# A two-pass decoder layer on eight cores: embedding-stage adds on Pool, new buffer places, a norm and the start loads moved

## What is computed

```python
def rmsnorm(x, g):
    return x * rsqrt(mean(x * x, axis=-1) + EPS) * g

def swiglu(x, w_gate, w_up, w_down):              # D_MODEL 1024, D_FF 2816
    return (silu(x @ w_gate) * (x @ w_up)) @ w_down

h = x + 0.5 * rmsnorm(swiglu(rmsnorm(x, g1), ...), g2)      # FFN 1
proj = rmsnorm(h, g3) @ w_in                                 # mixer: [b_a | c_a | h_a | u | v]
y_a = b_a * causal_dwconv3(c_a * h_a)
y_b = u * (tril(W_s) @ rmsnorm(v) + b_s)                     # over chunks of 128 positions
h = h + rmsnorm(concat(rmsnorm(y_a), rmsnorm(y_b)) @ w_out, g4)
h = h + 0.5 * rmsnorm(swiglu(rmsnorm(h, g5), ...), g6)      # FFN 2
gate = sigmoid(h @ ple_w_gate)                               # embedding stage
h = h + rmsnorm(gate * (p_emb @ ple_w_proj), g7)
```

## Time and profile before

| what | us |
|---|---|
| median of 3 runs | 1333.33 (1333.08 to 1335.34) |
| the profiled execution, its own time | 1332.94 |
| span of its slowest core, core 2 | 1331.8 |
| spans of all cores | 1326.5 to 1331.8 |
| busy in the span: PE, DVE, ACT, Pool | 1290.0, 524.1, 411.3, 94.7 |

### The profile page before, as it was taken

The page is one execution under the profiler, slowest core; times in us unless marked ns, Lnnn a source line. Parts: engine busy times, 40 slices in busy tenths (PEclk is TensorE's granted clock), DMA queues, the critical chain, the costliest instruction groups (busy, mean ns, idle before and its releaser), DMA issues.

```text
span 1331.8 us, 18723 instructions; the slowest of 8 cores (1326.5 to 1331.8 us)
## 1 busy us (share of the span) xinstructions
PE 1290.0 (97%) x6734; PEld 651.8 (49%) x6816; DVE 524.1 (39%) x694; ACT 411.3 (31%) x862; POOL 94.7 (7%) x185
## 2 busy tenths in 40 slices
PE   8999999999999999999998999999999999999995
PEld 6566664455545666654443344444444444444442
DVE  3222222447696222213266321223477922122237
ACT  3311112344465111111166211123334721111136
POOL 2110000001001100000001100000010011000000
PEclk9999999999999999999999899999999999999998
DMA  8999322129725963231289994332297299333123
GB/s 186 201 208 207 65 48 48 24 39 178 123 49 108 168 110 64 48 72 25 48 176 257 215 182 79 58 62 32 48 179 130 56 144 175 69 63 58 32 40 126
DMA packets 88906, 139.89 MB, mean 105 GB/s; under 512 B 58352, under 2 KB 58608, under 8 KB 88432
## 3 DMA queue, kind: packets, MB, share of 16 engines
q0 software_dynamic: 25296, 90.25, 41.1%
q1 hardware_dynamic: 63520, 48.43, 13.5%
HBM read 206.03 MB, written 9.51 MB: 162 GB/s over the span
## 4 chain that ended last, share of the span: by engine, by line
PE 85%; DVE 5%; ACT 4%; DMA 3%; issue 3%; SPq 0%; ACTq 0%; DVEq 0%
PE ps L212 56%; PE ps L557 24%; PE ps L546 3%; DVE nT L221 1%; DMA y<-big 1%; DMA nT<-nbr 1%; ACT big L217 1%; DMA h<-xT 1%; DVE big L225 1%; DVE big L221 1%; ACT sg L217 1%; DVE nbr L221 1%; ACT L217 1%; PE ps L711 1%; ACT nbr L217 1%
## 5 line engine op out<-in xcount | busy, mean ns | idle before, releaser
L212 PE MATMUL ps<-nT,ring 128*128 128x384 bf16 (+1 forms) x4127 | 776.6, 349 | 16.4 <-DVE nT L221 7.9
L212 PEld LDWEIGHTS ps<-nT,ring 128*128 128x128 bf16 x4160 | 407.9, 98 | 381.4 <-issue 29.4
L225 DVE TENSOR_TENSOR big<-ps,sg 128x384 bf16<-128x384 f32 (+1 forms) x220 | 134.0, 611 | 489.3 <-PE ps L212 469.8
L557 PE MATMUL ps<-ring,big 128*128 128x512 bf16 x1291 | 283.7, 379 | 1.5
L217 ACT ACTIVATE sg<-ps 128x384 f32<-128x384 f32 (+1 forms) x237 | 127.0, 537 | 500.9 <-PE ps L212 490.3
L557 PEld LDWEIGHTS ps<-ring,big 128*128 128x128 bf16 x1320 | 129.2, 98 | 155.5
L253 POOL DMA_DIRECT2D ring<-w x170 | 90.2, 539 | 1066.7 <-PE ps L212 461.5
L217 ACT ACTIVATE big<-ps 128x1024 bf16<-128x1024 f32 (+4 forms) x89 | 75.4, 862 | 226.3 <-PE ps L557 195.2
L225 DVE TENSOR_TENSOR zsc<-ps,gains 128x1024 f32<-128x1024 f32 x51 | 62.3, 1222 | 180.2 <-ACT big L217 180.1
L557 PE MATMUL ps<-ring,nT 128*128 128x512 bf16 x470 | 104.9, 379 | 2.1 <-DVE big L225 1.4
L557 PEld LDWEIGHTS ps<-ring,nT 128*128 128x128 bf16 x480 | 46.8, 98 | 58.3 <-issue 2.5
(11 more groups left out here) (73 smaller groups left out, 363.5 us busy)
## 6 DMA issues: line engine op xcount, KB each, us to landing
ring<-w POOLq DMA_DIRECT2D x170, 512.0 KB, 15.1
h<-x SPq DMA_DIRECT2D x17, 512.0 KB, 30.2
gains<-gain SPq DMA_DIRECT2D x12, 512.0 KB, 9.2
y<-big SPq DMA_DIRECT2D x12, 512.0 KB, 10.8
big<-xT SPq DMA_DIRECT2D x2, 2048.0 KB, 13.8
y<-zsc SPq DMA_DIRECT2D x4, 512.0 KB, 6.2
h<-xT SPq DMA_DIRECT2D x4, 384.0 KB, 5.9
h<-xT SPq DMA_DIRECT2D x2, 768.0 KB, 10.7
```

The lines of the kernel that those rows point to most:

```text
L212: ins = nc.tensor.matmul(out_ap, l, r, start=(i == 0), stop=(i == n - 1))
L225: return DVE.mark(nc.vector.tensor_tensor(out=out, in0=in0, in1=in1, op=op))
L557: ins = nc.tensor.matmul(o.t, lhs(k), sv, start=(k == 0), stop=(k == nk - 1))
```

## The change

The change has these parts.

1. **Pool adds.** In `ple` of pass 0 the residual add of blocks 0 to 5 is a Pool instruction that waits for DVE's multiply; the store waits for it.
2. **Places.** `gb(b)` of blocks 6, 7, 8 moves to columns 8192 and up of `big`. Their Sigmoid waits for `x_apply` of tile 0 of pass 1, which read there. `guard1` and `gb_guard` follow: the first rows now wait for the stores of blocks 0 to 3.
3. **Last norm.** `tok_stage` returns its last block's `pre` instead of doing it. After the down projection nothing changes hands, as there `pre` is not late. After the output projection it runs as a hook after the first unit of gate-and-up, with the gain loads, the load of `pT` and the owed fills that stood behind it.
4. **Start.** Tile 0 loads in two parts, tile 1 in one; Pool begins with the weights when tile 0 is there. Pass 0 starts with three pairs of `j` over tiles 0 and 1; the statistics of tile 2 stand one unit ahead of its first use.
5. **Second pass.** Groups of two in `ple`. The last group but one goes through `middle_two`: gain multiply while ACT has the statistics, then one `stt` for scale and add; tables are loaded ahead by one-element activations.

```diff
     def gb(b):
-        i = b % 6
-        return zsc_t[:, i - 4, :] if i >= 4 else bigf[:, 1024 * i:1024 * (i + 1)]
+        if b in (4, 5):
+            return zsc_t[:, b - 4, :]
+        o = 1024 * b if b < 4 else 8192 + 1024 * (b - 6)
+        return bigf[:, o:o + 1024]
...
-    xt_load(PASSES[0], 0, 4)
+    xt_load(PASSES[0], 0, 2)
     ev_gc = gc_sem.add(nc.sync.dma_start(out=gc_t[:], in_=gcol_d))
-    xt_load(PASSES[0], 1, 2)
+    xt_load(PASSES[0], 1)
...
-    POOL.wait(xt_ev[0, 1][0])
+    POOL.wait(xt_ev[0, 0][3])
     issue_next()
...
-        if pend is not None:
-            pre_fn(*pend)
-        return e
+        return pend
...
-            e = tt([e], gb(b), gb(b), h_t[:, b, :], ALU.add)
+            if N is not None and b < 6:
+                POOL.wait(e)
+                e = POOL.mark(nc.gpsimd.tensor_tensor(out=gb(b), in0=gb(b), in1=h_t[:, b, :], op=ALU.add))
+            else:
+                e = tt([e], gb(b), gb(b), h_t[:, b, :], ALU.add)
             out_ev[b] = store(b, e)
...
+        def zg_of(b):
+            return bigf[:, 4096 + 1024 * (b - 4):4096 + 1024 * (b - 3)]
+
+        def table(func):
+            nxt["tab"] = act([nxt.get("tab")], out=sv_t[:, 0, 0, 0:1], in_=ones_t[:, 0:1], func=func)
+
+        def middle_two(b0, b1):
+            for b in (b0, b1):
+                sigmoid(b, gate(b, False))
+            table(AF.Ln)
+            st = {}
+            for b in (b0, b1):
+                product(b, *embed(b, False))
+            for b in (b0, b1):
+                st[b] = rstd_of(gb(b), sg_t[:].rearrange("p a s -> p (a s)"), [zev[b]], D)
+                st[b] += (tt([zev[b], gain_ev[base + GPLE]], zg_of(b), gb(b), gain(base + GPLE), ALU.mult),)
+            table(AF.Sigmoid)
+            for b in (b0, b1):
+                r, e3, e1, ez = st[b]
+                out_ev[b] = store(b, stt([e3, e1, ez], gb(b), zg_of(b), r, h_t[:, b, :], ALU.mult, ALU.add))
...
     def gb_guard(b):
-        return [guards["zsc"] if b % 6 >= 4 else None, out_ev.get(b - 6) if b >= 6 else None]
+        if b in (4, 5):
+            return [guards["zsc"]]
+        return [xn_ev[1, 0][-1]] if b >= 6 and (1, 0) in xn_ev else []
...
             lo, hi = j * 576 // 1024, (j * 576 + 575) // 1024
-            evs = [out_ev.get(x + 6 if x < 3 else x) for x in range(lo, hi + 1) if x < 4]
-            if hi >= 4:
-                evs += [xn_ev[1, 1][-1], xn_ev[1, 0][-1]]
+            evs = []
+            for x in range(lo, hi + 1):
+                if x < 4:
+                    evs.append(out_ev[x])
+                elif x < 8:
+                    evs.append(xn_ev[1, 1][-1])
+                else:
+                    evs += [xn_ev[1, 0][-1], out_ev[x - 2] if x < 11 else None]
...
-            gu_stage(P, 2, guard1, {(1, 0): (1, start_square), (1, 1): (0, start_mid), (2, 0): (0, start_loads),
+            gu_stage(P, 3, guard1, {(1, 1): (1, start_square), (2, 0): (1, start_mid), (3, 0): (0, start_loads),
                                     (8, 0): (0, late_consts)},
-                     [(0, 0), (0, 1), (1, 0), (1, 1), (0, 2), (1, 2)])
+                     [(0, 0), (0, 1), (1, 0), (1, 1), (2, 0), (2, 1), (0, 2), (1, 2), (2, 2)])
...
+        def last_norm(P=P):
+            pre_ffn2(*pend)
+            gain_load(base + GPLE, [last_pre["ev"]])
+            gain_load(base + NGAIN + G1POST, [last_pre["ev"]])
+            POOL.wait(vo_last, last_pre["ev"])
...
+            pay_owed([nT_ev[P.nb - 1]])
+
+        gu_stage(P, 3, guard_none, {(0, 0): (1, last_norm)})
...
-        groups = [[0, 1, 2], [3, 4, 5], [6, 7, 8]] if P.nb == 9 else [[0, 1, 2], [3, 4, 5], [6, 7]]
+        groups = [[0, 1, 2], [3, 4, 5], [6, 7, 8]] if P.nb == 9 else [[0, 1], [2, 3], [4, 5], [6, 7]]
```

More of the change, by code:

```diff
@@ L894, in finish @@
                 h_free[b] = e
+        def zg_of(b):
[16 more added lines that the diff above has]
+                out_ev[b] = store(b, stt([e3, e1, ez], gb(b), zg_of(b), r, h_t[:, b, :], ALU.mult, ALU.add))
         def last_two(b0, b1):
-            zg = [bigf[:, 4096:4096 + D], bigf[:, 4096 + D:4096 + 2 * D]]
-            junk = bigf[:, 4096 + 2 * D:4096 + 3 * D]
+            zg = [zg_of(b0), zg_of(b1)]
+            junk = bigf[:, 10240:10240 + D]
             gp = gain(base + GPLE)
@@ L949, in ple @@
                 break
+            if N is None and gi == len(groups) - 2:
+                middle_two(*grp)
+                continue
             for b in grp:
@@ L1052, in build_program @@
         nT_ev.clear()
-        tok_stage(P, 8, 2, lambda b, k: nT_t[:, k, b * 128:(b + 1) * 128], lambda b: [norm_ev[b]],
-                  base + GMPOST, 1.0, 3, 0, pre_mid(base + G2PRE), {0: tail})
-        gain_load(base + GPLE, [last_pre["ev"]])
-        gain_load(base + NGAIN + G1POST, [last_pre["ev"]])
-        POOL.wait(vo_last, last_pre["ev"])
-        w = P.tiles[-1][0] + P.tiles[-1][1]
-        pT_ev = None
-        for i, r0 in enumerate(sorted(set([P.rows[0]] + ([P.rows[8]] if P.nb == 9 else [])))):
-            n = 1024 if i == 0 else 128
-            pT_ev = pt_sem.add(nc.gpsimd.dma_start(out=pT_v[:, :, i * 1024:i * 1024 + n], in_=pT_d[:, :, r0:r0 + n]))
-        pay_owed([nT_ev[P.nb - 1]])
-        gu_stage(P, 3, guard_none)
+        pre_ffn2 = pre_mid(base + G2PRE)
+        pend = tok_stage(P, 8, 2, lambda b, k: nT_t[:, k, b * 128:(b + 1) * 128], lambda b: [norm_ev[b]],
+                         base + GMPOST, 1.0, 3, 0, pre_ffn2, {0: tail})
+        ple_in = {}
+        def last_norm(P=P):
[3 more added lines that the diff above has]
+            POOL.wait(vo_last, last_pre["ev"])
+            for i, r0 in enumerate(sorted(set([P.rows[0]] + ([P.rows[8]] if P.nb == 9 else [])))):
+                n = 1024 if i == 0 else 128
+                ple_in["ev"] = pt_sem.add(nc.gpsimd.dma_start(out=pT_v[:, :, i * 1024:i * 1024 + n],
+                                                              in_=pT_d[:, :, r0:r0 + n]))
+            pay_owed([nT_ev[P.nb - 1]])
+        gu_stage(P, 3, guard_none, {(0, 0): (1, last_norm)})
+        pT_ev = ple_in["ev"]
         hold_fills(1)
```

## The result

The changed kernel takes **1315.86 us** (median of 4 runs, 1314.76 to 1316.48) against 1333.89 for the kernel before in the same comparison (4 runs, 1333.08 to 1335.34). The ratio is 0.9863, 95% interval 0.9846 to 0.9880. The prediction was 1315.5, within 1307 to 1322. The profiled execution took 1316.48 and has a span of 1315.4 on core 2, the slowest, as before.

A forecast was written before the change was run, and what follows sets the result against it. PE, busy 1290 of 1331.8 us, bounds the kernel, so only its waits and lower clock count. Terms -2.6 - 2.2 - 2.0 - 1.8 - 10.9 + 2.7 + 1.0 - 2.0 = -17.8 took 1333.3 to 1315.5, range 1307 to 1322.

The forecast's parts named there:

- Guards, -10.9: First gate-and-up of second pass: moved blocks 6 to 8 end the waits on stores, -10.9 of 11.3 us lost.
- Exclusion, +2.7 and +1.0: First pass's embedding stage: Pool's adds shut out DVE, PE's wait grows +2.7 us, lower clock behind it +1.0.
- rival (a): Embedding stage: Pool and DVE work side by side, +3.7 becomes -2.0, total 1309.8 us; chance 0.28.
- Start, tile 2 and clock, -6.8: First gate-and-up: earlier weights -2.6 us, more matmul cover at tile 2 -2.2, clock regained behind shorter idle spells -2.0.
- Last norm, -1.8: First pass, second gate-and-up: norm of block 8 moved behind the first unit removes PE's Silu wait, -1.8 us.
- Weight fills behind the adds: Pool queue, embedding stage: second and third fills wait for adds until about 696 and 716, just land, no cost.
- rival (b): After the embedding stage: weights behind the adds come late, PE stands up to 8 us, total 1323; chance 0.08.
- Tail, -2.0: Second pass's embedding stage: groups of two start the first product sooner, -2.0 us (0 to -4).
- Rivals (c) to (e): In order: start gains nothing, 1320; late fills stall PE, 1334 to 1340 (0.03); guard still waits, 1326 (0.11 with the first).
- (c): Start: tile 1 loses what the weights gain, clock stays low, +4.6, 1320 us; chance 0.11 shared with the guard-still-waits case.

The follow-up runs named there:

- the memsets: Changed kernel with Pool's six adds replaced by memsets of the same blocks, residual add left out: 1308.76 us, one run on another chip.
- fused: Changed kernel with all adds on DVE; blocks 0 to 2 multiply by the gain early, then one scale-and-add: 1310.13 us (0.9822); on another chip 1314.86 (0.9858).
- the kernel with late ones: Fused kernel with tile 0 in four parts, tile 1 in two, and weights waiting for tile 1's first half: 1316.98 us (0.9870).
- the three fused kernels of the last chip: Fused kernel again, 1314.86 us; with tile 0 in four parts and tile 1 in two, 1314.53; those pieces plus late weights, 1316.98.

## Why the prediction was right, point by point

**The time** came out to 0.4 us, but part of that is luck. The terms of the profiled pair sum to -16.4, not -17.8; its execution of the changed kernel was the longest of four, and the medians are 18.0 apart. On the other chip the same kernel was 15.1 below the kernel before, 2.7 less than predicted.

**Guards, -10.9:** -11.3. DVE no longer stands on the stores, tile 1 of pass 1 is ready in time, the clock is 1.00. Alone the part gives a ratio of 0.9923, 9.5 us.

**Exclusion, +2.7 and +1.0:** the mechanism and its place are shown by three kernels (adds back on DVE, Pool in the second group only, Pool without reads). The step of the sum was that multiplies, adds and normalisation follow one another in 15.7 us from the first multiply (684.34 to 700.0). It took 15.57 (677.52 to 693.09), with the adds on DVE 12.96, and with the memsets 9.79. The wait was put at 1.38 + 2.7 = 4.1 and is 3.98. The add was estimated at 2.15 us; alone it takes 2.36, and 3.0 on the mean of the two that meet DVE. The clock behind the wait was mis-sized on core 2: 16 matmuls lose 5.85 - 3.45 = 2.4, not 1.0, since the stretches 692 to 700 have 0.57 and 0.58, where the row it was taken from had 0.77. On six of the eight cores it was nearly right: they lose 1.3 to 1.7, and on core 0 the same stretches have 0.80 and 0.78. The whole term is +4.2 on core 2 and +3.2 on the median core, since the second wait, 0.66, is gone, as rival (a) also had it. The Trainium skill, "SBUF — State Buffer", section "Who interferes with whom", on the shared port pair, has a DVE instruction with two SBUF inputs and a GpSimd one that reads SBUF exclude each other. The traces agree: 4.52 for two multiplies beside adds, 1.28 each beside memsets, and 3.47 for three products with a PSUM input beside adds.

**Rival (a)** fell for the change as it stands, but its price was well taken: where the wait goes (memsets 1308.76, fused 1310.13), the time is about what it said, 1309.8, and the embedding stage is 2.3 shorter than before (41.1 for 43.4), where it had 2.0.

**Start, tile 2 and clock, -6.8:** -4.8 on core 2, -5.1 on the median core. The step that failed is "its squares and statistics ... end about 1 us later": the squares begin 3.4 later (16.85 for 13.46), so PE's first real matmul stays where it was, at 22.29, and not at 19.5. Still the early weights are worth 2 to 3 us, by the kernel with late ones: without them the cores that wait for the weights begin after 22 with a gap of 3.4 right ahead and the lower clock behind. In the change PE's gap is 1.3 and lies ahead of the statistics, with warm-up matmuls behind it, and from 24 us on the clock is 1.00, where it was 0.77. So a small part of the gain that I had booked as an earlier begin came as clock: the stage itself is 5.0 shorter on core 2 (174.5 for 179.5), where 2.2 + 2.0 were predicted; the other 2.0 of the -6.8 did not come. Tile 2 was right: 0.6 predicted to remain, 0.4 remains; with its clock the unit order alone gives 3.6.

**Last norm, -1.8:** -2.0, no wait left. No experiment undid it; the rows show it directly.

**Weight fills behind the adds:** the second and third groups of fills were put at 696 and 716 by the times of the kernel before, whose stage begins 7.1 later, so at 689 and 709; they went out at 688.51 and 707.99. PE never waits for the ring in the next stage, so rival (b) did not happen.

**Tail, -2.0:** -2.3, and the kernel with groups of three gives exactly that back.

**Rivals (c) to (e)** did not come: (c) was right in that PE does not begin sooner, wrong in that the clock stays low.

## What to carry to other kernels

Moving an elementwise step to Pool was free here only where nothing of PE waited for DVE, and it gained nothing there (1313.52 against 1313.21). Beside DVE instructions with two SBUF inputs, DVE loses nearly the whole length of Pool's; beside DVE instructions with an input in PSUM it loses nothing. Look for DVE's idle time instead: multiplying by the gain while ACT still has the statistics, and one fused scale-and-add after, gave 3 us where Pool's adds cost 3 to 4. And after a load was moved ahead, look at what shared its transfers: the piece size of the next tile took from PE's begin what the earlier weights gave.

## What the runs showed that was not expected

- **The granted clock falls to 0.81 without any idle PE.** In some executions and on some cores it does so between about 670 and 730 us, once for 5 to 15 us or several times for 5 to 10, at DMA shares near 1.0. It costs 1 to 6 us of span: core 4 of the fused kernel's second profile spends 2.1, 2.2 and 1.8 us more than core 2 in the embedding stage, the gate-and-up stage behind it and the rest. Other cores have the same instructions and the same DMA share at 1.00. By the profiled executions it accounts for most of why the change gave 0.9863 once and 0.9886 the second time, and the fused kernel 0.9822 and 0.9858.
- **What starts it stays open**, and no run was made on it. Four profiled executions have PE's wait of 4 us in the embedding stage (the change twice, its kernel with groups of three, Pool's adds on the kernel before); three of them have 0.81 on all eight cores, the first of the change on none. Of the ten without that wait, six have it nowhere, the moved places alone on cores 4 and 5, and the three fused kernels of the last chip on cores 4 to 7. So it may be that the wait makes it more likely, and that part of the 6.3 us is a price of Pool's adds after all; or it goes with the chip. No run separates the two.
- **A wait of 4 us costs 1.3 to 2.4 us more in clock**, by core: on cores 2 and 7 the 16 matmuls behind it take 5.8 to 5.9 for 3.45, on the six others 4.7 to 5.2. Behind a wait of 1.38 they take 3.45, with nothing lost.
- **Pool and DVE share the loss unevenly.** In the first group DVE lost 6.2 us (4.52 and 9.57 against 2.56 and 5.38) to three adds that take 7.1 alone; Pool's own two adds lost 1.3 (6.02 against 4.7).
- **A loss can hide in a later wait:** Pool's adds alone on the kernel before cost 2.1, since PE then waits less for the stores; on the changed kernel they cost 3 to 4.
- The fastest kernel that leaves nothing out has all other parts of the change and the fused first group: 0.9822 on one chip and 0.9858 on another, where the change has 0.9886 on the first. With the smaller pieces at the start it is 0.9857, not distinguishable.
